# Zero products ahead of the first loads' arrival, and a reordered set of first loads, in a two-block transformer kernel on one core

## The reference

```python
h = rmsnorm(x, attn_norm_w[l])      # y = x * rsqrt(mean(x*x) + eps) * w
proj = h @ w_in[l]
```

## Time and profile before

| | before |
|---|---|
| median of three runs | 2660.0 us (2658.65 to 2663.03) |
| the profiled execution, its own time | 2658.19 us |
| its span in the profile | 2656.4 us |
| TensorE busy | 2619.3 us, 99% of the span |
| VectorE, ScalarE, GpSimd busy | 60%, 39%, 15% |
| mean DMA rate over the span | 141 GB/s |

### The profile page before, as it was taken

How to read it: one execution, slowest core, us unless ns; L and a number is a source line. 1 busy time by engine, 2 the same in 40 slices (tenths; PEclk the granted TensorE clock), 3 DMA queues, 4 the chain that set the end, 5 groups by cost and what they waited for, 6 DMA issues and landing times.

```text
span 2656.4 us, 33800 instructions
## 1 busy us (share of the span) xinstructions
PE 2619.3 (99%) x12616; PEld 2116.1 (80%) x12616; DVE 1601.4 (60%) x2440; ACT 1028.5 (39%) x1334; POOL 410.3 (15%) x147
## 2 busy tenths in 40 slices
PE   8999999999999999999999999999999999999998
PEld 6767888888876778888888888888888888888886
DVE  4467211213999976579998988888344444444444
ACT  4465322214346763232223455555332222222223
POOL 0001455542010003424444000000000000000000
PEclk9999999999999999999999999999999999999999
DMA  5111222222222222223333365465565555555552
GB/s 184 48 48 69 97 102 97 99 95 95 95 84 76 68 80 96 95 95 145 148 142 143 135 230 192 186 233 201 198 229 189 189 189 191 195 197 195 194 196 95
DMA packets 121737, 374.37 MB, mean 141 GB/s; under 512 B 7553, under 2 KB 73217, under 8 KB 92737
## 3 DMA queue, kind: packets, MB, share of 16 engines
q1 hardware_dynamic: 117968, 333.74, 35.5%
q10 hardware_dynamic: 2016, 35.26, 3.4%
q0 software_dynamic: 1680, 4.46, 0.6%
HBM read 301.86 MB, written 69.21 MB: 140 GB/s over the span
## 4 chain that ended last, share of the span: by engine, by line
PE 83%; DVE 13%; issue 2%; ACT 2%; DMA 0%; DVEq 0%; POOL 0%; POOLq 0%; ACTq 0%
PE ps L1042 26%; PE ps L1044 25%; PE ps L1043 25%; PE ps L1552 2%; DVE cand_t L2179 1%; DVE z L1910 1%; DVE cand_t L2175 1%; DVE sel L2181 1%; DVE wl L1640 1%; DVE topi L2141 1%; DVE topi L2151 1%; DVE sc L2144 1%; DVE sel L2184 1%; DVE bpos L2141 1%; DVE bpos L2151 1%
## 5 line engine op out<-in xcount | busy, mean ns | idle before, releaser
L1042 PE MATMUL ps<-hh,wh 128*128 128x512 f32 x1968 | 783.3, 398 | 9.3 <-DVE wl L1646 8.0
L1044 PE MATMUL ps<-hh,wl 128*128 128x512 f32 x1968 | 768.8, 391 | 0.0
L1043 PE MATMUL ps<-hl,wh 128*128 128x512 f32 x1968 | 767.8, 390 | 0.0
L531 ACT ACTIVATE wh<-raw 128x2048 fp32r<-128x2048 f32 x217 | 414.9, 1912 | 771.2 <-PE ps L1044 769.9
L2208 DVE TENSOR_TENSOR wl<-raw,wh 128x2048 fp32r<-128x2048 f32 x101 | 231.3, 2290 | 432.8 <-ACT wh L531 432.8
L1042 PEld LDWEIGHTS ps<-hh,wh 128*128 128x128 f32 x1968 | 370.2, 188 | 98.9 <-issue 15.6
L1044 PEld LDWEIGHTS ps<-hh,wl 128*128 128x128 f32 x1968 | 370.0, 188 | 79.3
L1043 PEld LDWEIGHTS ps<-hl,wh 128*128 128x128 f32 x1968 | 370.7, 188 | 74.3 <-issue 1.0
L1042 PE MATMUL ps<-gah,wh 128*128 128x512 f32 x1024 | 398.7, 389 | 0.0
L1044 PE MATMUL ps<-gah,wl 128*128 128x512 f32 x1024 | 398.7, 389 | 0.0
L1043 PE MATMUL ps<-gal,wh 128*128 128x512 f32 x1024 | 398.7, 389 | 0.0
(11 more groups left out here) (259 smaller groups left out, 3006.8 us busy)
## 6 DMA issues: line engine op xcount, KB each, us to landing
raw<-in_w_slots SPq DMA_DIRECT2D x217, 1024.0 KB, 4.8
a_spill<-ast SPq DMA_DIRECT2D x64, 512.0 KB, 2.6
gate_table<-stage ACTq DMA_DIRECT2D x8, 4096.0 KB, 13.0
at<-a_spill SPq DMA_DIRECT2D x64, 512.0 KB, 5.8
tt<-gate_table SPq DMA_DIRECT2D x64, 512.0 KB, 6.8
lnb<-z POOLq DMA_DIRECT2D x36, 64.0 KB, 1.9
xT<-in_x SPq DMA_DIRECT2D x4, 512.0 KB, 7.2
bt<-in_rel_tiles POOLq DMA_DIRECT2D x1, 2048.0 KB, 12.2
```

The costliest lines, as they stand in the source:

```text
L531: act.activation(wh[:, b, :], raw[:, b, :], ACT.Copy).then_inc(sem("w_hi"), 1)
L1042: nc.tensor.matmul(bank, whi, xhi, start=start, stop=False)
L1043: nc.tensor.matmul(bank, whi, xlo, start=False, stop=False)
L1044: return nc.tensor.matmul(bank, wlo, xhi, start=False, stop=stop)
```

## The change

It adds four products on a cleared tile, `warm`, to the start of TensorE's program, and a clear of that tile to VectorE's; they write PSUM bank 5, and their result is never read. The load of `vec` is cut in two: the first eight columns come first (`gain_in`), the other 381 are issued from ScalarE's queue after the high part of slot 0's second piece, ahead of `cst`, and ScalarE waits for them ahead of `norm(0, 2)`. The first 512 columns of slot 0 are loaded from ScalarE's queue instead of SyncE's. Tiles 0 and 1 of x are loaded by two DMAs with a signal each.

```diff
+        warm = z1[:, ORDER1[-1], :]
         csc = (z1[:, 0:2, :], z1[:, 2:4, :], ab[:, 0:2, :])
...
-            x_pair(0)
-            sp.dma_start(raw[:, 0, 0:512], ins["w_slots"][0, :, 0:512]).then_inc(sem("w0_raw"), 16)
+            sp.dma_start(xT[:, 0, :], ins["x"][:, 0, :]).then_inc(sem("x_first"), 16)
+            sp.dma_start(xT[:, 1, :], ins["x"][:, 1, :]).then_inc(sem("x_in0"), 16)
             x_pair(1)
             sp.dma_start(raw[:, 0, 512:2048], ins["w_slots"][0, :, 512:2048]).then_inc(sem("w_raw0"), 16)
...
-            act.dma_start(vec[:, :], ins["vec"]).then_inc(sem("vec_in"), 16)
+            act.dma_start(vec[:, 0:KD], ins["vec"][:, 0:KD]).then_inc(sem("gain_in"), 16)
+            act.dma_start(raw[:, 0, 0:512], ins["w_slots"][0, :, 0:512]).then_inc(sem("w0_raw"), 16)
...
             ln_exp_tables()
-            act.wait_ge(sem("vec_in"), 16)
+            act.wait_ge(sem("gain_in"), 16)
...
             for k in range(KD):
-                if k % 2 == 0:
+                if k == 0:
+                    act.wait_ge(sem("x_first"), 16)
+                elif k == 1 or k % 2 == 0:
                     act.wait_ge(sem(f"x_in{k // 2}"), 16)
                 x_high(0, k)
                 if k == 0:
                     first_high("w0_raw", 0)
                 if k == 2:
                     first_high("w_raw0", 1)
+                    act.dma_start(vec[:, KD:], ins["vec"][:, KD:]).then_inc(sem("vec_in"), 16)
                     act.dma_start(cst[:, :, :], ins["cst"]).then_inc(sem("cst_in"), 16)
...
             high(2, 0)
+            act.wait_ge(sem("vec_in"), 16)
             norm(0, 2)
...
+            pe.wait_ge(sem("warm"), 1)
+            for _ in range(4):
+                nc.tensor.matmul(ps[:, 5, :], warm[:, 0:P], warm, start=True, stop=True)
             pe.wait_ge(sem("w0_lo"), 1)
...
+            dve.memset(warm, 0.0).then_inc(sem("warm"), 1)
             dve.sem_inc(sem("ev_pq"), 4)
```

## The result

The kernel became slower: 2663.74 us median of 22 runs (2661.84 to 2667.20) against 2659.19 of 22 runs before (2658.07 to 2663.27), ratio 1.0016, 95% interval 1.001 to 1.0022. That is 4.5 us slower. It is just under the 5.3 us that the prediction took as what can be told, and the time lies outside the range of the prediction. The profiled execution is longer by 6.4 us, a span of 2662.8 against 2656.4.

The account below looks back on a forecast made before the run. The prediction took TensorE, busy 99% of the span, to bound the kernel, with the start-up held by slot 0's second piece. Only that piece's 0.4 us counted: 2660.0 becomes 2659.6, range 2657.1 to 2662.1.

Parts of the forecast that it names:

- What bounds: TensorE's start-up: its end is set by when 768 KB land at about 9.6; a head start of twelve products runs into that.
- The new idle time: TensorE, after the first twelve products: idle from 10.0 to 12.5, some 2.5 us, until the second piece is split.
- The zero products: The four added products at TensorE's start: begin at 1.4, clock rises at 6.3, end at 7.3 (4.2 to 8.4).
- The first real product: TensorE's first product of slot 0: ready at 6.4 (5.6 to 8.0), starting behind the added products at 7.3.
- the term of 1.4 us: Loads ahead of the first real product: 446 KB fewer to land, worth 1.4 us (bounds nothing and 2.3).
- The second piece: Slot 0's second load: fewer bytes ahead, high part starts at 9.2, thirteenth product 0.4 us sooner (bounds 0 and 0.5).
- rival D: Changed loads do nothing for slot 0's second piece: 2660.0, chance 0.13; its sign, ScalarE's line 583 still at 9.6.
- Slots 1 and 2, vec's rest, the wait ahead of the norm: Later loads and splits stay covered: 1.3 us left for slot 1, 4 us for slot 2, 17 us for the norm.
- Rival A: Clock falls in TensorE's new gap before the thirteenth product: price 1.6 us, 2661.2, chance 0.15.
- Downstream: From 13 us on TensorE runs dense and later waits hang on its own products, so 0.4 us reach the end.
- rival E: Some other large effect (code layout, a later loop that falls otherwise), either way, chance 0.04.
- rivals A to D: Also includes: zero products fail to raise the clock, 2660.5, chance 0.10; whole 3.1 us head start counts, 2656.9, chance 0.04.

Follow-up runs that it names:

- e7: The changed kernel with one spare semaphore increment at the head of VectorE's program: 2659.83 us, ratio 1.0001.
- e2: The changed kernel with the clear of the tile on GpSimd instead of VectorE: 2659.11 us, ratio 0.9991.
- e3: The new order of the loads alone, the clear and four products taken out of the changed kernel: 2658.05 us, ratio 0.9994.
- e8: The changed kernel with two spare semaphore increments at the head of VectorE's program: 2664.97 us, ratio 1.0015.
- e11: The changed kernel with four unread products of constants in TensorE's wait before the selections are turned: 2662.10 us against 2658.62, ratio 1.001.
- e9: The kernel before with GpSimd's low parts cut to 8 of 2048 columns for the first 27 expert slots: 2658.44 us against 2658.62, ratio 0.9998.

## Why the prediction was wrong

*What bounds.* Right for the first 13 us in what it said of the first twelve: the first twelve products and the slow clock were worth nothing, and the wait of 0.21 us for the second piece was the row that told it. The new idle time came out at 2.01 us (forecast 2.5).

*The zero products.* Start 1.47 (1.4), end about 6.8 (7.3); the clock rose earlier than I had taken from the one rise in the trace. It rose later in e7, where the last of the eight records starts at 7.59 and not at 6.2 to 6.8. The first real product was ready at 7.86 in the execution after, later than my 6.4, and at 7.1 to 7.3 in e2, e3, e8 and e11. The high part of the first piece began at 6.45 as before, or at 5.7 to 5.9 in the other five traces with the new loads, so the term of 1.4 us was 0 to 0.7. No run moved that issue alone, so what the queue and what the bytes did stays open.

*The second piece.* Forecast 0.4 us sooner. The thirteenth product starts at 12.92, 12.37, 12.36, 12.52, 12.39 and 12.29 in the six executions with the new loads, and between 13.06 and 13.84 in the seven with the old. The middles are 0.76 us apart. The term was right in kind and too small. In the profiled execution itself the high part began at 9.59, which I had named as the sign of rival D; in the other five it began at 8.96 to 9.18.

*Slots 1 and 2, vec's rest, the wait ahead of the norm:* covered, as forecast; no wait of TensorE appears there.

*Rival A.* The fall of the clock in the new gap did not come in the execution after, but it did in e8: products from 13.08 on stood 0.43 us apart, after an idle time of 2.08. It can happen, at about the price given: at TensorE's wait near 685 us e8 is 1.5 to 1.7 us behind e2, e3, e7 and e11.

*Downstream: the step that failed.* I wrote that everything else in the program is left as it is and that from 13 us on only 0.4 us reach the end. I costed VectorE's clear only by its duration, in the start of the zero products, and put its effect on VectorE's later code at nothing, without a reason. It is not only an operation in time but also an instruction in the program: it moved all of VectorE's later code by one place, and the top-k search, which starts at 1175 us, lost 3.1 us. TensorE was waiting for that search already, 1.3 us; so all of it came through, and with the wait at 4.4 us the clock fell too. In the sum: −0.8 (loads), +3.1 (stops and GpSimd), +1.4 to 2.1 (clock), 3.7 to 4.4 us against 4.5 measured. My rival E named code layout, without a mechanism and with a chance of 0.04.

*Slips in the sums.* From the high part's start at 6.45 and 1.53 us behind it, a gain of 1.4 gives a first product at 6.6 and not 6.4; the bytes after are 2.10 MB. The forecast and rivals A to D have 0.96 together, where I wrote 0.94. None of this moves the forecast.

What stays open: that the stops are the fetching of code is inferred. For it speak their distance of 128 instructions, and the instruction queue q14: beside the search it moves exactly one packet of 8 KB for each unit, in the kernel after 0.7 to 2.9 us behind each of the eight stops, and as many in the kernel before. No run changed the fetch itself.

The Trainium skill bears on both. "Runtime: NRT & Kernel Launch", Instruction fetch mechanics, calls the crossing of a block of code mostly hidden; here the crossing, if it is that, costs 0.35 us where an operation stands at it and nothing where the wait behind a longer operation does. The page gives blocks of 16 KiB, 256 instructions; the stops here are 128 instructions apart, with packets of 8 KB. "SBUF — State Buffer", SBUF: two separate sides, says that VectorE's operations with two SBUF inputs and GpSimd's that read SBUF hold a shared port pair in turn, each for its whole length; the run e9 agrees, with 35 us, and the one-input `TENSOR_REDUCE` kept its 1220 ns throughout.

Of the versions that compute everything, the loads alone (2658.05) and the change with the clear on GpSimd (2659.11) have the lowest ratios, 0.9994 and 0.9991; their intervals reach 1.0003 and 1.0, so a gain of 1 to 2 us is likely and not shown.

## What to carry to other kernels

Ask of every added instruction not only when it runs but what straight code stands behind it on its engine, and whether anyone waits for that code; a try with one spare instruction more or less tells a change of position from a change of work. A head start pays only up to the next wait in the row: look for the product that was released last, not for the first. Where one engine's long wait decides, see which of its operations stand still for another engine's.

## What the runs showed that was not expected

- One semaphore increment, of no use, at the head of VectorE's program costs 4.5 us of 2660; two cost nothing (ratios 1.0016 and 0.9999).
- The stops are 0.35 us each and 128 instructions apart, at the same instruction numbers in all kernels; behind an operation of 1.2 us they do not show.
- GpSimd's subtraction of 4.6 us holds VectorE's two-input operations for up to 4.2 us: 35 of the 280 us of the top-k search. Which operation its last one catches makes the whole difference of 3.1 us between the two parities.
- An idle time of 2.60 us near 765 us left the clock high in the execution before, 2.61 us at the same place in that after did not, nor did 2.08 us in e8: the length of the idle time alone does not decide whether it falls. After 4.42 us it fell in all five kernels with an odd count and no filler.
